# Layer 0 of a diffusion block: the last features ahead of two norms made in two token halves, each half with a norm of its own

## The chip, the cores and the metric

One core of a Trainium2 chip. The metric is device time in microseconds of one execution of the whole program, the median of the runs. The program has two parts, a two-layer transformer block on query and context tokens (the "first block") and a two-layer recurrent block; the change touches the first one alone, mostly its layer 0.

## What is computed

Query tokens `x` (256 x 1024) and context tokens `ctx` (256 x 1024), float32. Layer `l` of the first block:

```python
hx = modulate(rms_norm(x, norm_mix_g[l]), sh_a, sc_a)        # hc likewise from ctx
y_x, y_c = even_mixer(...)                                   # l = 0: two attentions
# l = 1: odd_mixer: q from hx alone, k and v from hx and hc
x = x + g_a * (y_x @ w_out[l])
x = x + g_f * swiglu(modulate(rms_norm(x, norm_ffn_g[l]), sh_f, sc_f), ffn_w_in[l], ffn_w_out[l])
# l = 0: the same two updates for ctx, with the gates and shifts of c_ctx
```

`rms_norm` divides each token by the root of the mean of its 1024 squared features, so it can begin only when the last feature of the token is there. `modulate(h, sh, sc)` is `h * (1 + sc) + sh`; all `sh`, `sc`, `g` come from a product of the condition with `mod_w` (the "modulation"), 12 column blocks of 512 per layer.

## The kernel before

**Products in three passes.** Every float32 product is made of fp32r parts: `hi*hi + hi*lo + lo*hi` (`product`, lines 505 to 509). A weight chunk is 512 inputs x 512 outputs (1 MB). SyncE loads it into `raw`, a ring of `RING = 4` slots; ScalarE writes its high part into `w_hi`, a ring of `HI_RING = 3` (line 1190); VectorE writes the low part over the raw one (line 1639). SyncE may load chunk c only when chunk c-4 is used:

```python
if c >= RING:
    sp.wait_ge(*projected.after("used", c - RING))
```

All chunks stand in one list in the order in which TensorE takes them (`lay_out`, line 2468, must name the same order as the program of TensorE). Modulation chunks are in the same list and ring; they are used raw (`mod_chunk`, line 797: one chunk of 4 kt, recorded as 8 matmuls at line 815) and need no split. `mod_row` (line 830) hangs two of them behind every second weight chunk of layer 0; `among(..., 2)` in `lay_out` is the same rule on the host side. Four modulation chunks fill one bank (5 or 6); ScalarE copies it (`modulation`, line 1340), TensorE turns it (`mod_turn`, line 781, bank 4), VectorE adds the bias (line 1870).

**Order written out by hand.** Each engine has one program. On TensorE layer 0 ends with `project_feat("w_out", 0, 2, ...)`, `root_of_squares`, `swiglu(0, 4)`, `root_of_squares`, `od_q`, `od_kv` (lines 941 to 947). A chunk of `project_feat` with all 512 tokens is 4 slabs of 128 output features x 4 kt x 3 passes = 48 matmuls with 512 columns; a slab has a PSUM bank of its own (0 to 3). Two chunks (1024 inputs) make 512 output features. `od_q` takes the 256 query tokens only (24 matmuls a chunk); `od_kv` takes 512 tokens as two groups of two token tiles. Before a product overwrites a bank, `claim` waits for the instruction that reads it last (for `od_q` and `od_kv` that is VectorE's copy in `store`, line 1927).

**The way through a norm.** For each finished slab VectorE updates the residual `X` (`residual`, lines 1891 to 1924, one 128x256 instruction for queries and one for context), ScalarE squares it (line 1219), VectorE adds the square to a sum over features (line 1674). After the last slab: `root_of_squares` (line 614) sums over the partitions, ScalarE takes the root (line 1252), VectorE the reciprocal and a diagonal matrix (lines 1690, 1691), TensorE spreads it over all partitions (line 623, bank 7). Then, per feature block k of 128 features and all 512 tokens: VectorE scales (line 1699), ScalarE applies the modulation (line 1268, twice) and writes the high part (line 1262), VectorE writes the low part (line 1704). The next product takes the blocks one by one. The low parts of weight chunks stand among this on VectorE (`lo_to`, line 1632), the high parts on ScalarE (`split_to`, line 1181), both in the order of the list.

**Names of chunks.** Around the first place: w0 to w3 are the four chunks of `w_out` (two output halves of two chunks), f0, f1, ... those of `ffn_in` (two per column block), m a modulation chunk. The last part of `ffn_out` has two output halves with one chunk of 4 kt and one of 2 kt each; q0 to q3 are the chunks of `od_q`.

## Time and profile before

| | us |
|---|---|
| median of 3 runs | 2416.76 |
| lowest, highest | 2415.67, 2419.11 |
| profiled execution | 2416.47 |
| its span, first to last instruction | 2414.7 |
| TensorE busy | 2304.4 |
| VectorE, ScalarE busy | 1503.6, 1013.3 |
| mean granted clock, share of full speed | 0.982 |

PE is TensorE, PEld its weight loads, DVE VectorE, ACT ScalarE, SPq the queue in which SyncE issues loads. A row of a timeline gives start and duration; in square brackets stands how long the engine was idle before it and whose instruction ended that. Durations of matmuls are longer than their distance, since they overlap: the distance of two starts is their cost.

### The profile page before, as it was taken

Reading aid. Unit: us, or ns where it says so; the run is one execution under the profiler, and the core shown is the slowest. Engines: PE = TensorE matmul, PEld = TensorE weight load, DVE = VectorE, ACT = ScalarE, POOL = GpSimd, SP = SyncE. Lnnn points to the kernel's source line nnn. Section 1 sums busy time; section 2 is a strip of 40 time slices with the busy share of each in tenths; the row PEclk is TensorE's granted clock in tenths of the full one; section 3 lists DMA queues with packets and bytes.
Section 4 is the critical chain, followed back from the end, with each engine's and each line's share of the span. In section 5 each row is a group of like instructions: output and inputs, shape, how many; then the busy total and the mean of one; then the engine's idle time right before and its main releaser. Section 6 shows DMA issues by size and latency. Waiting matters only on the chain.

```text
span 2414.7 us, 33051 instructions
## 1 busy us (share of the span) xinstructions
PE 2304.4 (95%) x14198; PEld 1985.0 (82%) x14198; DVE 1503.6 (62%) x1866; ACT 1013.3 (42%) x1226; POOL 0.2 (0%) x4
## 2 busy tenths in 40 slices
PE   6988989999998887999999999999999999999997
PEld 3765767777876756999999877999989988789997
DVE  3777443333356577555678767675668767767475
ACT  4255441111224155434664345443456534444343
POOL 0000000000000000000000000000000000000000
PEclk9999999999998999999999999999999999999999
DMA  8530134444332241455555453555545445445552
GB/s 324 206 143 1 54 137 176 177 172 181 133 117 93 87 105 71 158 184 192 216 191 187 174 193 143 179 188 176 189 177 205 179 174 197 148 175 177 190 176 104
DMA packets 61401, 389.19 MB, mean 161 GB/s; under 512 B 6600, under 2 KB 11080, under 8 KB 16072
## 3 DMA queue, kind: packets, MB, share of 16 engines
q1 hardware_dynamic: 61256, 387.08, 44.0%
q8 instruction: 112, 1.84, 0.3%
q14 instruction: 33, 0.27, 0.0%
HBM read 386.01 MB, written 1.05 MB: 160 GB/s over the span
## 4 chain that ended last, share of the span: by engine, by line
PE 84%; DVE 8%; ACT 4%; DMA 2%; issue 2%; SPq 0%; DVEq 0%; ACTq 0%
PE PS L507 26%; PE PS L508 25%; PE PS L509 25%; DMA raw<-chunks_in 2%; PE PS L815 1%; PE PS L984 1%; DVE w_lo L1639 1%; ACT w_hi L1190 1%; DVE stat L1838 1%; PE PS L694 1%; PE PS L966 1%; ACT xn L1268 1%; PE PS L654 1%; PE PS L719 1%; DVE BIG L1847 1%
## 5 line engine op out<-in xcount | busy, mean ns | idle before, releaser
L1639 DVE TENSOR_TENSOR w_lo<-raw,w_hi 128x2048 fp32r<-128x2048 f32 x300 | 683.5, 2290 | 514.4 <-ACT w_hi L1190 512.5
L1190 ACT ACTIVATE w_hi<-raw 128x2048 fp32r<-128x2048 f32 x300 | 571.7, 1912 | 755.7 <-PE PS L509 453.3
L507 PE MATMUL PS<-x_hi,w_hi 128*128 128x256 f32 (+1 forms) x2048 | 629.0, 307 | 12.2 <-DVE x_lo L1704 7.8
L509 PE MATMUL PS<-x_hi,w_lo 128*128 128x256 f32 (+1 forms) x2048 | 626.1, 306 | 0.0
L508 PE MATMUL PS<-x_lo,w_hi 128*128 128x256 f32 (+1 forms) x1984 | 601.5, 303 | 0.0
L507 PEld LDWEIGHTS PS<-x_hi,w_hi 128*128 128x128 f32 x2048 | 393.6, 192 | 38.5 <-issue 21.8
L509 PEld LDWEIGHTS PS<-x_hi,w_lo 128*128 128x128 f32 x2048 | 393.6, 192 | 16.7
L508 PEld LDWEIGHTS PS<-x_lo,w_hi 128*128 128x128 f32 x1984 | 381.7, 192 | 14.1
L507 PE MATMUL PS<-w_hi,x_hi 128*128 128x512 f32 (+1 forms) x800 | 318.5, 398 | 23.2 <-DVE x_lo L1704 12.0
L508 PE MATMUL PS<-w_lo,x_hi 128*128 128x512 f32 (+1 forms) x800 | 314.5, 393 | 0.0
L509 PE MATMUL PS<-w_hi,x_lo 128*128 128x512 f32 (+1 forms) x800 | 313.9, 392 | 0.0
L507 PE MATMUL PS<-BIGR,w_hi 128*128 128x256 f32 (+1 forms) x896 | 272.8, 304 | 0.0
L508 PE MATMUL PS<-BIGR,w_hi 128*128 128x256 f32 (+1 forms) x896 | 272.3, 304 | 0.0
L509 PE MATMUL PS<-BIGR,w_lo 128*128 128x256 f32 (+1 forms) x896 | 272.3, 304 | 0.0
L507 PEld LDWEIGHTS PS<-w_hi,x_hi 128*128 128x128 f32 x800 | 152.6, 191 | 63.2 <-issue 18.8
L507 PEld LDWEIGHTS PS<-BIGR,w_hi 128*128 128x128 f32 x896 | 171.3, 191 | 10.4 <-issue 3.6
L509 PEld LDWEIGHTS PS<-w_hi,x_lo 128*128 128x128 f32 x800 | 152.5, 191 | 31.8
L508 PEld LDWEIGHTS PS<-w_lo,x_hi 128*128 128x128 f32 x800 | 152.6, 191 | 29.7
L509 PEld LDWEIGHTS PS<-BIGR,w_lo 128*128 128x128 f32 x896 | 171.3, 191 | 6.9
L508 PEld LDWEIGHTS PS<-BIGR,w_hi 128*128 128x128 f32 x896 | 171.3, 191 | 6.7
L507 PE MATMUL PS<-w_hi,BIGR 128*128 128x512 f32 x192 | 75.7, 394 | 0.0
L509 PE MATMUL PS<-w_hi,BIGR 128*128 128x512 f32 x192 | 74.8, 390 | 0.0
(298 smaller groups left out, 2281.2 us busy)
## 6 DMA issues: line engine op xcount, KB each, us to landing
raw<-chunks_in SPq DMA_DIRECT2D x348, 1024.0 KB, 4.8
bias_ring<-brows_in SPq DMA_DIRECT2D x32, 256.0 KB, 5.1
G<-nrows_in SPq DMA_DIRECT2D x2, 1536.0 KB, 6.6
free_b<-rel_in SPq DMA_DIRECT2D x4, 512.0 KB, 7.8
BIG<-rel_in SPq DMA_DIRECT2D x4, 512.0 KB, 8.7
tabt<-tabs_in SPq DMA_DIRECT2D x1, 1536.0 KB, 12.6
X<-x_in SPq DMA_DIRECT2D x1, 1024.0 KB, 8.7
X<-ctx_in SPq DMA_DIRECT2D x1, 1024.0 KB, 10.7
```

The costliest lines, as they stand in the source:

```text
L507: pe.matmul(o, lhs[0], rhs[0], start=start, stop=False, **more)
L508: pe.matmul(o, lhs[0], rhs[1], start=False, stop=False, **more)
L509: return pe.matmul(o, lhs[1], rhs[0], start=False, stop=stop, **more)
L654: mm = pe.transpose(PS[:, bank, t * P:(t + 1) * P], src(b, t), ident)
L694: mm = pe.matmul(PS[:, s + i, 0:d["nk"]], a, b, start=m == 0, stop=m == len(mats) - 1)
L719: mm = pe.matmul(PS[:, b, 0:P], pT_, val, start=j == 0, stop=j == n - 1)
L815: mm = pe.matmul(PS[32 * kt:32 * kt + 32, b, :], cond[:, 4 * kg + kt, at:at + 32], w[:, kt, :], start=first, stop=i == last and kg == 1, s ...
L966: mm = pe.matmul(PS[:, b, cols], qkT[:, 8 + 2 * h + j, s * P:(s + 1) * P], qkT[:, 2 * h + j, s * P:256], start=j == 0, stop=j == 1)
L984: mm = pe.matmul(PS[:, 6 + t, 0:dv], lhs, val[:, s, h * dv:(h + 1) * dv], start=s == 0, stop=s == len(blocks) - 1)
L1190: act.activation(w_hi[:, i % HI_RING, :], ring[:, n % RING, :], ACT.Copy).then_inc(*hi_ready.now(n))
L1268: ins = act.activation(o, o, ACT.Identity, bias=modc[l][:, kind * 8 + k, w:w + 1], scale=modc[l][:, kind * 8 + 8 + k, w:w + 1])
L1639: dve.tensor_tensor(w_lo[:, c % RING, :], ring[:, c % RING, :], w_hi[:, i % HI_RING, :].bitcast(F32), ALU.subtract).then_inc(*lo_ready.now(c))
```

## The change

Both places, end of `w_out` into `ffn_in` and end of `ffn_out` into `od_q`, are treated alike. The last 512 output features are made for the query tokens first (banks 0, 1) and then for the context tokens (banks 5, 6), from the same two chunks, which are held until both are done. Each half has its own squares, sum, root and spread (banks 7 and 4, two columns and 256 columns), its own scaling and its own high and low parts. The first column block of `ffn_in` is made for the queries, block by block, then for the context, again from held chunks; `od_q` begins with the query blocks, and the second group of `od_kv` waits for the context blocks. Scale, reciprocal root and low part are now two VectorE instructions of 256 columns with the modulation's factor in them, the high part one ScalarE instruction. In the first place the modulation chunks are moved: four behind w1 and four behind f3, instead of two behind w1, w3, f1 and f3. The low half of `y4T`, `krT` and a buffer of modulation rows lie elsewhere, and `ffn_in` reads its activations from other memory.

The core of the diff (order and names; left out are the new buffers' places, the semaphore counters and waits that follow from these):

```diff
-        y4T = pair_of((xhi_, xnr_), 512, KD)
+        y4T = pair_of((xhi_, bigr(8192, 4096)), 512, KD)
+        hT_f0 = pair_of((xlo_, xnr_), 512, KD)
...
+            def project_halves(st, j, rhs, k_tiles, hooks):
+
+                parts, held = range(-(-k_tiles // KC)), []
+                for who in range(2):
+                    for kg in parts:
+                        if who == 0:
+                            held.append(take_chunk(st, 0))
+                        c, w = held[kg]
+                        for s in range(4):
+                            bank, at = half_banks[who][s // 2], s % 2 * 256
+                            if kg == 0 and at == 0:
+                                claim(bank)
+                            for kt in range(KC * kg, min(KC * kg + KC, k_tiles)):
+                                mm = product(PS[:, bank, at:at + 256], [a[:, kt - KC * kg, s * P:(s + 1) * P] for a in w],
+                                             [a[:, kt, who_cols(who)] for a in rhs], kt == 0 and at == 0, kt == k_tiles - 1, True)
+                            if kg == parts[-1] and at:
+                                mm.then_inc(*projected.now(st, 0, j, (who, s // 2)))
+                                reader[bank] = x_ready.after(st, 0, j, (who, s // 2))
+                            elif who == 1 and s == 3:
+                                mm.then_inc(*projected.now(("chunk", c)))
+                            if who == 1 and s == 3:
+                                used(c)
+                            if (who, kg, s) in hooks:
+                                hooks[who, kg, s]()
+                plan[("last chunk", st, 0, j)] = c
...
+            def first_halves(st, rhs, tiles_of, freed, hooks):
+
+                held = []
+                claim(0, 1, 2, 3)
+                for who in range(2):
+                    for kg in range(2):
+                        if who == 0:
+                            held.append(take_chunk(st, 0))
+                        c, w = held[kg]
+                        for kt in range(KC * kg, KC * kg + KC):
+                            pe.wait_ge(*copied_v.after(tiles_of, (who, kt)))
+                            for s in range(4):
+                                mm = product(PS[:, s, who_cols(who)], [a[:, kt - KC * kg, s * P:(s + 1) * P] for a in w],
+                                             [a[:, kt, who_cols(who)] for a in rhs], kt == 0 and who == 0, kt == KD - 1, True)
+                                if who == 1 and kt == KD - 1:
+                                    mm.then_inc(*projected.now(st, 0, 0, s))
+                                    reader[s] = freed(0, s)
+                            if who == 1 and kt == KC - 1:
+                                mm.then_inc(*projected.now(("chunk", c)))
+                            if (who, kt) in hooks:
+                                hooks[who, kt]()
+                        if who == 1:
+                            used(c)
+                plan[("last chunk", st, 0, 0)] = c
...
+            def half_sums(key, who):
+
+                acc, bank = sums[4][0], (7, 4)[who]
+                pe.wait_ge(*x_summed.after(key, (who, KD - 1)))
+                claim(bank)
+                for t in range(2):
+                    mm = pe.matmul(PS[:, bank, t:t + 1], acc[:, (2 * who + t) * P:(2 * who + t + 1) * P], tab("ones")[:, 0:1],
+                                   start=True, stop=True)
+                mm.then_inc(*sums_bc.now(key, who))
+
+            def half_spread(key, who):
+
+                bank = (7, 4)[who]
+                pe.wait_ge(*rstd_diag.after(key, who))
+                pe.matmul(PS[:, bank, 256:512], tab("ones"), sums[4][2][0][:, who_cols(who)], start=True,
+                          stop=True).then_inc(*rstd_bc.now(key, who))
+                reader[bank] = scaled.after(key, who, KD - 1)
...
+            def mod_four(kg):
+
+                for _ in range(4 * kg):
+                    mod_chunk()
...
+                    if halves:
+                        first_halves("ffn_in", hT_f0, ("ffn", 0), freed,
+                                     {(0, 1): lambda: half_sums(("ffn", 0), 1), (0, 3): lambda: half_spread(("ffn", 0), 1)})
+                        tiles_of = None
+                        project_feat("ffn_in", 0, 1, hT_f0, n0=1, between=mod_four, width=width, freed=freed)
...
+                        project_feat("ffn_out", 0, 1, ffT[0], n0=2 * part, k_tiles=2 * n, width=width, freed=updated("ffn_out", 0),
+                                     need=lambda kg: hidden.after("ffn", 0, 2 * n0 + min(KC * kg + KC, 2 * n) - 1))
+                        project_halves("ffn_out", 2 * part + 1, ffT[0], 2 * n,
+                                       {(1, 0, 1): lambda: half_sums(("mix", 1), 0), (1, 0, 3): lambda: half_spread(("mix", 1), 0)})
+                        continue
...
-            project_feat("w_out", 0, 2, y4T, width=512, freed=updated("w_out", 0), need=copied("y0"), between=mod_row)
-            mod_end(0, 2)
-            root_of_squares(("ffn", 0), 4)
+            project_feat("w_out", 0, 1, y4T, width=512, freed=updated("w_out", 0), need=copied("y0"), between=mod_four)
+            project_halves("w_out", 1, y4T, KD,
+                           {(0, 1, 0): lambda: mod_end(0, 2), (1, 0, 1): lambda: half_sums(("ffn", 0), 0),
+                            (1, 0, 3): lambda: half_spread(("ffn", 0), 0)})
             swiglu(0, 4)
-            root_of_squares(("mix", 1), 4)
-            project_tok("od_q", 1, 2, KD, tokens(hT[4]), 1, tiles_of=("mix", 1))
-            project_tok("od_kv", 1, 4, KD, tokens(hT[4]), 2)
+            mix = ("mix", 1)
+            project_tok("od_q", 1, 1, KD, tokens(hT[4]), 1, tiles_of=mix)
+            project_tok("od_q", 1, 1, KD, tokens(hT[4]), 1, n0=1,
+                        between=lambda kg: half_sums(mix, 1) if kg == 0 else half_spread(mix, 1))
+            project_tok("od_kv", 1, 4, KD, tokens(hT[4]), 2, need_second=lambda: copied_v.after(mix, (1, KD - 1)))
...
+            def half_high(key, to, who, k0, k1):
+
+                l, kind = key[1], 0 if key[0] == "mix" else 3
+                for k in range(k0, k1):
+                    act.wait_ge(*scaled.after(key, who, k))
+                    act.activation(to[0][:, k, who_cols(who)], full[4][:, k, who_cols(who)], ACT.Identity,
+                                   bias=modc[l][:, kind * 8 + k, who:who + 1]).then_inc(*copied_s.now(key, who, k))
...
-            for k in range(KD):
-                act.wait_ge(*x_ready.after("w_out", 0, k // 4, k % 4))
+            for k in range(4):
+                act.wait_ge(*x_ready.after("w_out", 0, 0, k))
                 square(("ffn", 0), 4, k)
-                if k == 3:
-                    split_to(first + 3)
-                    split_to(first + 4)
             modulation(3)
-            root_mod(("ffn", 0), 4)
-            norm_mod(("ffn", 0), 4, 2, lambda: split_to(first + 5))
+            split_to(first + 3)
+            split_to(first + 4)
+            ffn = ("ffn", 0)
+            half_squares(ffn, "w_out", 1, 0)
+            act.wait_ge(*mods_ready.after(0, 2))
+            half_root(ffn, 0)
+            split_to(first + 5)
+            half_high(ffn, hT_f0, 0, 0, 2)
+            half_squares(ffn, "w_out", 1, 1, (0,))
+            half_high(ffn, hT_f0, 0, 2, 4)
+            half_squares(ffn, "w_out", 1, 1, (1,))
+            half_high(ffn, hT_f0, 0, 4, 6)
+            half_root(ffn, 1)
+            half_high(ffn, hT_f0, 0, 6, 8)
+            split_to(first + 6)
+            half_high(ffn, hT_f0, 1, 0, 8)
             swiglu(0, 4)
-            for k in range(KD):
-                if k % 4 == 0:
-                    split_for("ffn_out", 0, 4 + k // 4)
-                act.wait_ge(*x_ready.after("ffn_out", 0, 4 + k // 4, k % 4))
-                square(("mix", 1), 4, k)
-            root_mod(("mix", 1), 4)
-            norm_mod(("mix", 1), 4, 0)
+            mix, first_od = ("mix", 1), place_of[plan["first chunk", "od_q", 1]]
+            for k in range(4):
+                if k == 0:
+                    split_to(first_od - 2)
+                act.wait_ge(*x_ready.after("ffn_out", 0, 4, k))
+                square(mix, 4, k)
+            split_to(first_od)
+            half_squares(mix, "ffn_out", 5, 0)
+            act.wait_ge(*mods_ready.after(1, 0))
+            half_root(mix, 0)
+            split_to(first_od + 1)
+            half_high(mix, hT[4], 0, 0, 4)
+            split_to(first_od + 2)
+            half_high(mix, hT[4], 0, 4, 8)
+            half_squares(mix, "ffn_out", 5, 1)
+            split_to(first_od + 3)
+            half_root(mix, 1)
+            split_to(first_od + 4)
+            half_high(mix, hT[4], 1, 0, 8)
...
+                def scale(k):
+                    dve.scalar_tensor_tensor(full[4][:, k, cols], X[:, who, k, :], modc[l][:, kind * 8 + 8 + k, who:who + 1], r,
+                                             ALU.mult, ALU.mult).then_inc(*scaled.now(key, who, k))
+
+                if k0 == 0:
+                    dve.wait_ge(*rstd_bc.after(key, who))
+                    dve.wait_ge(x_ready.sem, x_ready.count)
+                    scale(0)
+                for k in range(k0, k1):
+                    if k + 1 < KD:
+                        scale(k + 1)
+                    dve.wait_ge(*copied_s.after(key, who, k))
+                    dve.scalar_tensor_tensor(to[1][:, k, cols], full[4][:, k, cols], modc[l][:, kind * 8 + k, who:who + 1],
+                                             to[0][:, k, cols].bitcast(F32), ALU.add, ALU.subtract).then_inc(*copied_v.now(key, (who, k)))
...
-            steps = {(0, 0): 12, (1, 0): 13, (1, 1): 14}
-            residual("w_out", 0, 2, 0, ("ffn", 0), lambda j, i: lo_to(ev + steps.get((j, i), 0)))
-            norm_mod(("ffn", 0), 4, 2, (0, 2), lambda k: lo_to(ev + 15) if k == 5 else None)
-            swiglu(0, 4, ("mix", 1))
-            norm_mod(("mix", 1), 4, 2, None, lambda k: lo_for("ffn_out", 0, 5) if k == 3 else None)
+            first = place_of[plan["first chunk", "w_out", 0]]
+            ffn, mix = ("ffn", 0), ("mix", 1)
+            residual("w_out", 0, 2, 0, ffn, lambda j, i: lo_to(first + 2), 1)
+            lo_to(first + 3)
+            half_update(ffn, "w_out", 1, 2, 0, 0)
+            half_adds(ffn, 0, 0)
+            modulation(0, 2)
+            lo_to(first + 4)
+            half_update(ffn, "w_out", 1, 2, 0, 1)
+            half_adds(ffn, 0, 1)
+            half_diag(ffn, 0)
+            half_low(ffn, hT_f0, 0, 0, 1)
+            lo_to(first + 5)
+            half_low(ffn, hT_f0, 0, 1, 2)
+            half_update(ffn, "w_out", 1, 2, 1, 0)
+            half_adds(ffn, 1, 0)
+            half_low(ffn, hT_f0, 0, 2, 3)
+            half_update(ffn, "w_out", 1, 2, 1, 1)
+            half_low(ffn, hT_f0, 0, 3, 4)
+            half_adds(ffn, 1, 1)
+            half_low(ffn, hT_f0, 0, 4, 6)
+            half_diag(ffn, 1)
+            half_low(ffn, hT_f0, 0, 6, 8)
+            half_low(ffn, hT_f0, 1, 0, 4)
+            lo_to(first + 6)
+            half_low(ffn, hT_f0, 1, 4, 8)
+            swiglu(0, 4, mix)
+            first_od = place_of[plan["first chunk", "od_q", 1]]
+            lo_to(first_od - 1)
+            half_update(mix, "ffn_out", 5, 5, 0, 0)
+            half_adds(mix, 0, 0)
+            lo_to(first_od)
+            half_update(mix, "ffn_out", 5, 5, 0, 1)
+            half_adds(mix, 0, 1)
+            half_diag(mix, 0)
+            half_low(mix, hT[4], 0, 0, 4)
+            lo_to(first_od + 1)
+            half_low(mix, hT[4], 0, 4, 8)
+            lo_to(first_od + 2)
+            for b in range(2):
+                half_update(mix, "ffn_out", 5, 5, 1, b)
+                half_adds(mix, 1, b)
+            lo_to(first_od + 3)
+            half_diag(mix, 1)
+            lo_to(first_od + 4)
+            half_low(mix, hT[4], 1, 0, 8)
...
-        among(weight_chunks(i["w_out"][l]), 2)
+        if l == 0:
+            w_out = weight_chunks(i["w_out"][0])
+            chunks.append(w_out[0:2])
+            mod_next(4)
+            chunks.append(w_out[2:4])
+        else:
+            chunks.append(weight_chunks(i["w_out"][1]))
         n0 = 0
         for n in FF_PARTS[l]:
-            among(weight_chunks(paired(i["ffn_w_in"][l])[:, 512 * n0:512 * (n0 + n)]), 2)
+            w_in = weight_chunks(paired(i["ffn_w_in"][l])[:, 512 * n0:512 * (n0 + n)])
+            if l == 0 and n0 == 0:
+                chunks.append(w_in[0:4])
+                mod_next(4)
+                w_in = w_in[4:]
+            among(w_in, 2)
             among(weight_chunks(i["ffn_w_out"][l][256 * n0:256 * (n0 + n)]), 2)
             n0 += n

```

`half_update`, `half_adds`, `half_diag`, `half_squares` and `half_root` are the steps of the norm above for one half: two updates, two adds, reciprocal and diagonal of 256 columns, two squares, one root of two columns.

## Rows read from the trace of the kernel before

**Rows 1.** The page, part 1: busy time of each engine.

```profile
PE 2304.4 (95%) x14198; PEld 1985.0 (82%) x14198; DVE 1503.6 (62%) x1866; ACT 1013.3 (42%) x1226; POOL 0.2 (0%) x4
```

**Rows 2.** Stretches of 20 us: PE, PEld, DVE, ACT, POOL busy, PEclk, DMA share, GB/s.

```profile
320.00:340.00 20.00, 12.28 (x54) 8.99 (x47) 11.46 (x22) 14.73 (x27) 0.00 (x0) 0.74 0.38 155
720.00:740.00 20.00, 9.73 (x28) 6.64 (x27) 13.27 (x25) 12.47 (x24) 0.00 (x0) 0.66 0.14 53
```

**Rows 3.** Whom TensorE waited for: us in total, times, longest.

```profile
PE PS L507 <- DVE x_lo L1704: 19.8, 5, 5.5
```

**Rows 4.** TensorE in order of time, end of `w_out`: start, us, what.

```profile
318.75 1.92 PE L815 MATMUL PS<-raw,bias_ring 128*32 128x512 f32 x16
...
331.59 0.77 PE L507 MATMUL PS<-x_hi,w_hi 128*128 128x512 f32 x1 [5.24 <-DVE x_lo L1704]
...
336.31 0.39 PE L509 MATMUL PS<-x_hi,w_lo 128*128 128x512 f32 x1
```

**Rows 5.** The chain that ended last, 270 to 420 us: start, us, what.

```profile
294.94 1.85 PE PS L815 x16
...
307.98 4.77 DMA raw<-chunks_in
...
355.75 1.85 PE PS L815 x16
...
379.63 1.85 PE PS L815 x16
381.49 0.43 PE PS L507
```

**Rows 6.** TensorE in order of time, end of `ffn_out`, start of `od_q`.

```profile
720.66 0.39 PE L509 MATMUL PS<-BIGR,w_lo 128*128 128x512 f32 x1
...
735.26 0.77 PE L507 MATMUL PS<-w_hi,x_hi 128*128 128x512 f32 x1 [4.29 <-DVE x_lo L1704]
...
744.89 0.47 PE L507 MATMUL PS<-w_hi,x_hi 128*128 128x512 f32 x1 [2.21 <-DVE x_lo L1704]
```

**Rows 7.** VectorE in order of time, `od_q` and `od_kv` being stored.

```profile
763.13 1.22 DVE L1935 COPY BIG<-PS 128x1024 f32<-128x1024 f32 x1 [1.14 <-PE PS L509]
...
833.14 2.35 DVE L1935 COPY BIG<-PS 128x1024 f32<-128x1024 f32 x2
```

**Rows 8.** TensorE at the last `od_kv` column block.

```profile
834.50 0.77 PE L507 MATMUL PS<-w_hi,x_hi 128*128 128x512 f32 x1 [6.13 <-DVE BIG L1935]
```

**Rows 9.** Weight splits, from the page's part 5: xcount, busy, mean ns.

```profile
L1639 DVE TENSOR_TENSOR w_lo<-raw,w_hi 128x2048 fp32r<-128x2048 f32 x300 | 683.5, 2290 | 514.4 <-ACT w_hi L1190 512.5
L1190 ACT ACTIVATE w_hi<-raw 128x2048 fp32r<-128x2048 f32 x300 | 571.7, 1912 | 755.7 <-PE PS L509 453.3
```

**Rows 10.** Chunk loads of 104 to 108 us, asked by line.

```profile
L1154 SPq DMA_DIRECT2D raw<-chunks_in x2: 328/328/328, 105.1 to 106.1; - x2
...
DMA to landing us min/median/max: 4.9/5.8/6.6
```

**Rows 11.** One modulation chunk on TensorE, same stretch.

```profile
105.00 1.07 PE L815 MATMUL PS<-raw,bias_ring 128*32 128x512 f32 x8
```

**Rows 12.** The split that waited for the second of those loads.

```profile
112.74 1.92 ACT L1190 ACTIVATE w_hi<-raw 128x2048 fp32r<-128x2048 f32 x1 [5.66 <-DMA raw<-chunks_in]
```

**Rows 13.** TensorE, matmuls of 512 columns back to back.

```profile
341.99 0.39 PE L507 MATMUL PS<-x_hi,w_hi 128*128 128x512 f32 x1
...
349.92 0.39 PE L509 MATMUL PS<-x_hi,w_lo 128*128 128x512 f32 x1
```

**Rows 14.** TensorE, matmuls of 256 columns back to back.

```profile
979.78 0.28 PE L507 MATMUL PS<-x_hi,w_hi 128*128 128x256 f32 x1
...
983.98 0.28 PE L509 MATMUL PS<-x_hi,w_lo 128*128 128x256 f32 x1
```

**Rows 15.** VectorE, residual update of 128x256, two instructions.

```profile
316.93 0.87 DVE L1910 SCALAR_TENSOR_TENSOR X<-PS,bias_ring,X 128x256 f32<-128x256 f32 x2
```

**Rows 16.** ScalarE, affine step of 128x256, four instructions.

```profile
328.13 2.07 ACT L1268 ACTIVATE xn<-xn,bias_ring 128x256 f32<-128x256 f32 x4 [4.05 <-DVE small L1889]
```

More of the change, by code:

```diff
@@ L541, in project_tok @@
                                 for kt in range(KC * kg, min(KC * kg + KC, k_tiles)):
+                                    if tiles_of == ("mix", 1) and j == n0 and t == 0:
+                                        pe.wait_ge(*copied_v.after(tiles_of, half(kt)))
                                     mm = product(PS[:, 2 * pair + t, 0:width], lhs(kt, 2 * g + t),
@@ L920, in swiglu, with freed @@
                 for part, n in enumerate(FF_PARTS[l]):
-                    project_feat("ffn_in", l, n, hT[tiles], n0=n0, tiles_of=tiles_of, between=between, width=width,
-                                 freed=lambda j, i: (unit_acted if i < first_u else stored).after("ffn_in", l, j, i))
+                    halves = l == 0 and part == 0
+                    def freed(j, i):
+                        return (unit_acted if i < first_u else stored).after("ffn_in", l, j, i)
+                    if halves:
[3 more added lines that the diff above has]
+                        project_feat("ffn_in", 0, 1, hT_f0, n0=1, between=mod_four, width=width, freed=freed)
+                    project_feat("ffn_in", l, n - 2 * halves, hT[2] if l else hT_f0, n0=n0 + 2 * halves, tiles_of=tiles_of, between=between,
+                                 width=width, freed=freed)
                     last = part == len(FF_PARTS[l]) - 1
@@ L1253, in root_mod, with half_squares, half_root @@
                                scale=1.0 / D).then_inc(*std_ready.now(key))
+            def half_squares(key, st, j, who, banks=(0, 1)):
+                for b in banks:
+                    act.wait_ge(*x_ready.after(st, 0, j, (who, b)))
+                    for k in (4 + 2 * b, 5 + 2 * b):
+                        act.wait_ge(*x_summed.after(key, k - 2 if b == 0 else (who, k - 2)))
+                        act.activation(sums[4][2][k % 2][:, who_cols(who)], X[:, who, k, :],
+                                       ACT.Square).then_inc(*x_squared.now(key, (who, k)))
+            def half_root(key, who):
+                act.activation(stat[:, 20:21], eps, ACT.Sqrt)
+                act.wait_ge(*sums_bc.after(key, who))
+                act.activation(stat[:, 2 * who:2 * who + 2], PS[:, (7, 4)[who], 0:2], ACT.Sqrt, bias=eps,
+                               scale=1.0 / D).then_inc(*std_ready.now(key, who))
+            def half_high(key, to, who, k0, k1):
[4 more added lines that the diff above has]
+                                   bias=modc[l][:, kind * 8 + k, who:who + 1]).then_inc(*copied_s.now(key, who, k))
             def norm_mod(key, tiles, part, middle=None):
@@ L1717, in norm_mod, with half_update @@
                         at_tile(k)
+            def half_update(key, st, j, kind, who, b):
+                dve.wait_ge(*projected.after(st, 0, j, (who, b)))
+                for s in range(2):
+                    k = 4 + 2 * b + s
+                    ins = dve.scalar_tensor_tensor(X[:, who, k, :], PS[:, half_banks[who][b], 256 * s:256 * s + 256],
+                                                   gate(0, kind, k, who), X[:, who, k, :], ALU.mult, ALU.add)
+                ins.then_inc(*x_ready.now(st, 0, j, (who, b)))
@@ new lines, in half_adds, with half_diag @@
+            def half_adds(key, who, b):
+                acc, _, sq = sums[4]
+                for k in (4 + 2 * b, 5 + 2 * b):
+                    dve.wait_ge(*x_squared.after(key, (who, k)))
+                    dve.wait_ge(*x_summed.after(key, 3 if k == 4 else (who, k - 1)))
+                    o = acc[:, who_cols(who)]
+                    dve.tensor_tensor(o, o, sq[k % 2][:, who_cols(who)], ALU.add).then_inc(*x_summed.now(key, (who, k)))
+            def half_diag(key, who):
+                dve.wait_ge(*std_ready.after(key, who))
+                r = stat[:, 4 + 2 * who:6 + 2 * who]
+                link(dve.reciprocal(r, stat[:, 2 * who:2 * who + 2]))
+                dve.tensor_tensor(sums[4][2][0][:, who_cols(who)].rearrange("p (t d) -> p t d", t=2),
+                                  ident.unsqueeze(1).to_broadcast([P, 2, P]), r.unsqueeze(2).to_broadcast([P, 2, P]),
+                                  ALU.mult).then_inc(*rstd_diag.now(key, who))
@@ L1897, in residual @@
                 before = []
-                for j in range(2):
+                for j in range(n):
                     for i in range(2 if l else 4):
@@ L1964, in swiglu @@
                         modulation(1, 0)
-                    if part == len(FF_PARTS[l]) - 1:
+                    if part == len(FF_PARTS[l]) - 1 and l == 0:
+                        first_od = place_of[plan["first chunk", "od_q", 1]]
+                        residual("ffn_out", 0, 5, 2 * part, key, lambda j, i: lo_to(first_od - 2), 1)
+                    elif part == len(FF_PARTS[l]) - 1:
                         residual("ffn_out", l, 5, 2 * part, key)
```

22 lines of the change are left out of this document (16 added, 6 removed).

## The prediction, made before the changed kernel ran

> **What bounds the kernel now.** The page says that TensorE is busy 95% of the span [rows 1]: what a stage is worth is the time for which TensorE stands still in it, or runs at half clock. The stretches of 20 us show two holes beside this change, at 320 and at 720 us, with 12.3 and 9.7 us of work at a granted clock of 0.74 and 0.66 [rows 2]. The view of waits names the releaser: VectorE's low half of the normed activations, 19.8 us in 5 waits [rows 3]. The timelines give the sizes. *First hole:* `w_out` and its two modulation chunks end at 320.7, the first `ffn_in` matmul starts at 331.6, and the next ten run at 0.43 us each, which is 1.2 GHz, where 0.227 is 2.4 GHz; they are through at 336.3 [rows 4, 13]. That is 10.9 us of standstill and 2.0 lost to the clock, **12.9**. *Second hole:* `ffn_out` ends at 720.9, `od_q` starts at 735.3 (14.4 us), pauses again before 744.9 (2.2 to 2.4 us), and both restarts pay some 1.8 for the clock [rows 6]: **20.4**.
>
> **What it costs in matmuls.** The last 512 features of each stage and the first `ffn_in` block go over 256 tokens at a time. 36 matmuls of 512 columns take 7.93 us from the first start to the last, 0.227 each [rows 13], 36 of 256 columns 4.20 us, 0.120 each [rows 14]. A split costs 2 x 0.120 - 0.227 = 0.013 us, for 96 + 96 + 72 = 264 matmuls: 3.4 us, 2.5 of them in the first stage. The Trainium skill ("TensorE: Matmul & The Clock Gate", Back-to-back issue gap) gives 518 cycles for 512 columns and 262 for 256, with which the split would cost 0.0025 us each and 0.7 in all. The rows decide.
>
> **The moved modulation chunks, first place.** Before, the order is w0 w1 m m w2 w3 m m f0 f1 m m f2 f3 m m f4. After, it is w0 w1 m m m m w2 w3 f0 f1 f2 f3 m m m m f4. The raw ring has four slots, so a load is issued when the chunk four places earlier is used. With T the end of w1 (294.9, [rows 5]), the fourth m is issued at T (its slot is w1's) and w2 only when the first m is done. Exactly this pair of loads exists in the trace: a chunk ends at 105.0, one load goes out at 105.1, a modulation chunk takes 1.07 us, the next load goes out at 106.1, and the second needs 6.6 us, since it shares the engines with the first: the split that waits for it starts at 112.74, 7.7 after the first chunk's end [rows 10 to 12]. So w2 lands at T+7.7, ScalarE's high part takes 1.91 and VectorE's low part 2.29 [rows 9], T+11.9. Behind this low part, by the new order, VectorE has the first residual update, 0.87 [rows 15], which frees PSUM bank 0: w2 starts at **T+12.8**. Before, it started at T+1.9 (two mods, 294.94 + 1.85). Four mods take 3.8 us, the rest TensorE stands, and I charge one restart at half clock, 2.0 as at 331.6. A single load without a queue lands after 4.77 us [rows 5]. The Trainium skill ("DMA: Bandwidth & Descriptors", Anatomy of one DMA) has about 2.0 us plus bytes over 436 GB/s, by which an estimate for the second of two 1 MiB loads is 6.8 us after the first's issue instead of 7.6; each restart would then come 0.8 earlier.
>
> **From w2 to the end of f1.** ScalarE splits w2 before it squares, VectorE updates four banks behind w2's low part (about 5.2 us with the adds), and only then comes w3's split: squares done T+16.3, mod row copied 16.9, high 18.8, low T+21.1. TensorE needs w3 at T+20.5: 0.7 lost. Query half of w3 done T+27.7 (with the modulation turn, 0.9, inside). VectorE meanwhile has the update, two adds, the modulation and f0's low part (2.29) ahead of the second update, so the query squares are summed at T+31.9, while the sum wants to start two slabs into the context half, T+30.5: 1.4 lost. The spread of the inverse roots comes two slabs later and waits for nothing; small products are 0.3 and 0.65 per half. The query half of the norm now runs beside the context half of w3, as it should: per feature block 2 VectorE instructions of 0.4 [rows 15] and one ScalarE of 0.52 [rows 16], block 0 ready at T+38.0, when TensorE is free at T+41.4. So **the hole of 12.9 goes**. What is late next: the context sums. VectorE has f1's low part, both context updates, adds and four query blocks ahead of them: T+46.4, wanted at T+44.2: 2.2 lost. After that each block is ready before its turn. Sum of the stretch T to the start of f2: 12.8 + 2.0 + 0.7 + 1.4 + 2.2 + 46.1 (384 half matmuls) + 2.8 (small products) = 68.0, T+68.0. Before it is 355.75 + 1.85 = 357.6 [rows 5], T+62.7. **+5.3 us.** The removed hole and four mods (16.7) are paid back by the w2 wait.
>
> **Second place.** f2 and f3 take 21.8, then come four mods again, with F the end of f3: the fourth issued at F, f4 at F+1.1, landed F+7.7, ready F+11.9. Before, two mods: F+1.9 [379.63 to 381.49, rows 5]. **+10.0**, and a restart at half clock, **+2.0**. ScalarE and VectorE wait for f4 in order ahead of the SiLU and product of block 1, but these are done by F+13, before bank 2 is wanted. First stage: 5.3 + 12.0 = **+17.3**. From f4 on TensorE is bound by itself, so nothing of this is made up.
>
> **Third place, `ffn_out` to `od_q`.** Here no modulation chunk is left. The residual of the first half no longer waits behind the low part of the last chunk, w3's counterpart is ready at 710.3 for a use at 710.2. The query sums are 2.1 us late (q0's low part sits between the two updates), TensorE ends `ffn_out` at 724.7 instead of 720.9, and goes on at once: query blocks come ahead of `od_q`, whose first pass ends at 735.6 and second at 747.2, the spread at 747.8. Hole of 20.4 gone. But a new wait: `od_kv` claims banks 0 and 1, which hold `od_q`'s first block, and VectorE stores that only behind all eight context blocks (8 x 0.8 + 0.6 from the spread on): 755.0 + 1.2 for the copy = 756.2. TensorE stands **8.5 us**, plus 2.0 at half clock. Its first `od_kv` chunk ends at 769.2. Before: the last `od_q` store at 763.1 [rows 7] follows the end of `od_q`, plus 10.9: 774.0. **-4.8.** Downstream the last `od_kv` block waits 6.13 us for a store [rows 8] that is behind the key norm on VectorE [rows 7]; that chain begins when the second `od_kv` block is done, so it moves with TensorE by the same 4.8. If it moves less, the gain is 3; were the 2.0 not paid, 7.
>
> **Sum.** The profiled execution is 2416.47, its span 2414.7, the median of the runs 2416.76. 2416.5 + 17.3 - 4.8 = 2429.0; to the median 0.3 more. I say **2429**. Unknown: what short stops (0.7, 1.4, 2.2, 2.1 us) do to the clock. The nearest row is the stop before 744.9, which cost 1.8: from 0 to 4 x 1.8 = 7.
>
> **Rivals.** *A (0.60):* as above, 2424 to 2434. *B, clock (0.17):* the short stops each cost a spell of 1.2 GHz: 2429 + 7 = 2436. For it: the 2.2 us stop before 744.9. *C, the small surplus (0.13):* VectorE is faster through the norm halves than I count, the late sums (0.7 + 1.4 + 2.2 + 2.1) vanish and the wait for the store halves (4.2 + clock 2): 2429 - 12.6 = 2416 to 2421; this is within 0.2% of before. *D, faster (0.10):* the loads behind the mods are hidden after all, because they go out before the first m is used. Then w2 starts at T+3.8 + 0.9 and f4 at F+3.8: 8.1 + 8.1 us less, and 4.0 of clock, 2409. It decides at one point: whether w2 and f4 can be issued at T and F or before. Against it: slot and program order, and the pair at 105 us.
>
> **Numbers.** About 0.2% (4.8 us) is what a measurement can tell from no change. Faster by more than it has D: 0.10. Within it, C and part of A's edge: 0.12. Slower: 0.78. The range leaves out D and the tails of B: 2417 to 2438.
>
> **What would show it.** TensorE waiting for a low weight part some 9 us at about 298 to 307 and again near 387 to 396, with ScalarE's split behind a DMA; after `od_q` a wait of about 8 us for a VectorE copy; no wait for x_lo over 1 us. It is wrong if the two waits behind the mods are under 4 us, or if the first stage (end of w1 to start of f4, 86.6 us now) is not some 17 longer.

## The result, and the profile after

| | before | after |
|---|---|---|
| median, us | 2416.23 | 2433.93 |
| single runs | 2415.67, 2415.69, 2416.76, 2419.11 | 2429.62, 2431.58, 2436.29, 2437.04 |
| profiled execution | 2416.47 | 2429.62 |
| its span | 2414.7 | 2427.8 |

The changed kernel takes 1.007 times as long (95% interval 1.0058 to 1.0082): slower by 17.7 us. The forecast was 2429, with a range of 2417 to 2438. A fourth run of the kernel before is counted here, so its median is 2416.23 and not the 2416.76 of its first three.

Part 1 of the page after; the counterpart is [rows 1]:

```profile
PE 2307.9 (95%) x14466; PEld 2000.0 (82%) x14466; DVE 1510.5 (62%) x1910; ACT 1005.3 (41%) x1222; POOL 0.2 (0%) x4
```

TensorE is busy 3.5 us longer, with 268 matmuls more. The profiled execution is 13.2 us longer, so the greater part of that is standstill, and the waits tell more. Whom TensorE waited for after (us in total, times, longest), against [rows 3]:

```profile
PE PS L514 <- DVE w_lo L1791: 15.0, 10, 5.0
PE PS L514 <- DVE BIG L2134: 14.4, 2, 8.3
PE PS L896 <- DMA raw<-chunks_in: 11.7, 6, 5.5
...
PE PS L514 <- DVE x_lo L1856: 7.7, 2, 5.2
...
PE PS L662 <- DVE G L1887: 6.5, 3, 2.5
...
PE PS L514 <- DVE X L2109: 5.7, 1, 5.7
```

The waits for the normed activations are gone from both places; what is left of `x_lo` stands at the start of the kernel (5.2) and in the next layer (2.6). In their place stand a weight low part (5.0), a residual update (5.7), two modulation chunks that wait for a load (4.5 of the 11.7; the other 7.1 stand in the first 60 us, as the 7.2 of the kernel before do), sums of squares (6.5), and VectorE's copy of `od_q` out of PSUM (8.3).

**The wait behind the first four modulation chunks.** TensorE in order of time (start, us, what, idle before):

```profile
291.49 2.78 PE L896 MATMUL PS<-raw,bias_ring 128*32 128x512 f32 x24
296.64 1.94 PE L896 MATMUL PS<-raw,bias_ring 128*32 128x512 f32 x8 [2.37 <-DMA raw<-chunks_in]
304.23 0.55 PE L514 MATMUL PS<-x_hi,w_hi 128*128 128x256 f32 x1 [5.66 <-DVE X L2109]
```

and the chain that ended last through the same stretch (start, us, what):

```profile
291.56 1.04 PE PS L896 x8
...
292.62 6.43 DMA raw<-chunks_in
...
299.07 1.92 ACT w_hi L1295
...
301.01 0.04 DVE w_lo L1791
...
303.22 0.88 DVE X L2109 x2
```

Read it from the bottom: w2 begins when the first residual update has freed its bank; the update stands behind w2's low part on VectorE; that waits for the high part, this for the load, and the load begins at 292.62, when the *first* modulation chunk is used, not at 291.56. The row of w2's low part (`w_lo`) is short because the chain leaves it at once: VectorE works on it from 301.01 for 2.29 us, and the update follows at 303.22. The fourth modulation chunk, issued at 291.59 into w1's slot, is itself late by 2.4 us, and takes 1.94 instead of 1.07, since the granted clock is half from 296.7. Behind w2's start the clock stays at half to 310.3: 28 matmuls of 256 columns run at 0.213 us each, where 0.120 is full speed. Before, the same point had 1.9 us of modulation between w1 and w2 and no wait (the first row of [rows 5] is this modulation).

**The same at the second four.** The chain again; here f4 waits for its own low part, and begins at 395.28:

```profile
383.65 1.04 PE PS L896 x8
...
384.71 6.26 DMA raw<-chunks_in
...
390.99 1.92 ACT w_hi L1295
...
392.93 2.30 DVE w_lo L1791
...
395.28 0.80 PE PS L514
```

**Third place.** TensorE waits for the sums of the query half, and then at the start of `od_kv`:

```profile
734.62 0.61 PE L662 MATMUL PS<-tabt,G 128*128 128x1 f32 x4 [2.51 <-DVE G L1887]
...
773.34 0.76 PE L514 MATMUL PS<-w_hi,x_hi 128*128 128x512 f32 x1 [8.26 <-DVE BIG L2134]
...
847.19 0.77 PE L514 MATMUL PS<-w_hi,x_hi 128*128 128x512 f32 x1 [6.13 <-DVE BIG L2134]
```

The last row is the wait that the kernel before has too [rows 8]. VectorE shows why the wait at 773.34 is 8.3 us: it is busy with the context blocks and copies `od_q` only behind the last of them.

```profile
765.12 0.87 DVE L1904 SCALAR_TENSOR_TENSOR xn<-X,bias_ring,PS 128x256 f32<-128x256 f32 x2 [2.40 <-PE PS L670]
...
771.57 0.48 DVE L1915 SCALAR_TENSOR_TENSOR x_lo<-xn,bias_ring,x_hi 128x256 fp32r<-128x256 f32 x1 [0.18 <-ACT x_hi L1381]
771.97 1.22 DVE L2134 COPY BIG<-PS 128x1024 f32<-128x1024 f32 x1
```

**Where the time went.** Three marks stand in every trace: T, the end of w1 (where two modulation chunks were moved ahead of w1, less their 1.9 us); M, the start of the modulation chunks behind f5; K, the first matmul of the last `od_kv` block [rows 8].

| | T | T to M | M to K |
|---|---|---|---|
| before | 294.9 | 108.6 | 431.1 |
| after | 291.5 | 127.6 | 428.2 |
| spread, first place | 292.9 | 121.9 | 430.1 |
| spread, second place | 294.0 | 117.6 | 429.8 |
| spread, both | 293.6 | 114.2 | 430.0 |
| third place alone | 294.7 | 108.7 | 431.4 |
| `od_q` stored early | 295.4 | 129.3 | 425.8 |
| low parts later | 297.2 | 125.1 | 425.9 |
| all repairs | 294.7 | 109.0 | 420.8 |
| third place alone, repaired | 293.6 | 109.6 | 420.9 |

After against before: +19.0 and -2.9, and from K to the end +0.4. The profiled execution also reached T 3.4 us earlier; T scatters from 291.5 to 297.2 over kernels that differ only behind it (the changed one, second place, `od_q` stored early, low parts later), so I count that as scatter and not as the change. Without it the sum is +16.5, close to the +17.7 of the medians; the single execution (+13.2) flatters the change.

### The profile page after: what moved, and what is told of

Its sections match the earlier page's. It is cut to its first block, busy times and chain, and to the rows that moved or that the text cites. A ratio compares the mean times of both kernels' runs of the same rounds, so it can differ in the third digit from the quotient of the medians.

```text
span 2427.8 us, 33640 instructions
## 1 busy us (share of the span) xinstructions
PE 2307.9 (95%) x14466; PEld 2000.0 (82%) x14466; DVE 1510.5 (62%) x1910; ACT 1005.3 (41%) x1222; POOL 0.2 (0%) x4
## 4 chain that ended last, share of the span: by engine, by line
PE 82%; DVE 9%; ACT 4%; DMA 2%; issue 2%; SPq 0%; DVEq 0%; ACTq 0%
PE PS L514 25%; PE PS L515 25%; PE PS L516 25%; DVE w_lo L1791 2%; ACT w_hi L1295 1%; DMA raw<-chunks_in 1%; PE PS L1089 1%; PE PS L896 1%; DVE stat L2037 1%; PE PS L1071 1%; PE PS L775 1%; PE PS L735 1%; PE PS L800 1%; DVE BIG L2046 1%; DVE PS L2035 0%
## 5 line engine op out<-in xcount | busy, mean ns | idle before, releaser
L514 PE MATMUL PS<-x_hi,w_hi 128*128 128x256 f32 (+1 forms) x1728 | 496.6, 287 | 12.6 <-DVE X L2109 5.7
L516 PE MATMUL PS<-x_hi,w_lo 128*128 128x256 f32 (+1 forms) x1728 | 494.7, 286 | 0.0
L515 PE MATMUL PS<-x_lo,w_hi 128*128 128x256 f32 x1632 | 463.0, 284 | 0.0
L514 PEld LDWEIGHTS PS<-x_hi,w_hi 128*128 128x128 f32 x1728 | 334.1, 193 | 17.1 <-issue 8.0
L516 PEld LDWEIGHTS PS<-x_hi,w_lo 128*128 128x128 f32 x1728 | 333.9, 193 | 1.3
L515 PEld LDWEIGHTS PS<-x_lo,w_hi 128*128 128x128 f32 x1632 | 314.5, 193 | 0.4
L515 PE MATMUL PS<-BIGR,w_hi 128*128 128x256 f32 (+1 forms) x1016 | 308.3, 303 | 0.0
L514 PE MATMUL PS<-BIGR,w_hi 128*128 128x256 f32 (+1 forms) x920 | 277.4, 301 | 0.1
L515 PEld LDWEIGHTS PS<-BIGR,w_hi 128*128 128x128 f32 x1016 | 195.6, 193 | 7.1
L514 PEld LDWEIGHTS PS<-BIGR,w_hi 128*128 128x128 f32 x920 | 175.9, 191 | 9.6 <-issue 3.4
L515 PE MATMUL PS<-xn_r,w_hi 128*128 128x512 f32 (+1 forms) x448 | 162.1, 362 | 0.0
L514 PE MATMUL PS<-x_lo,w_hi 128*128 128x512 f32 (+1 forms) x384 | 145.4, 379 | 5.0 <-DVE w_lo L1791 5.0
```

Source lines behind the costliest of these rows:

```text
L514: pe.matmul(o, lhs[0], rhs[0], start=start, stop=False, **more)
L515: pe.matmul(o, lhs[0], rhs[1], start=False, stop=False, **more)
L516: return pe.matmul(o, lhs[1], rhs[0], start=False, stop=stop, **more)
```

## The experiments

The theory: the four-slot ring makes w2 and f4 late behind four modulation chunks, this costs about 10 us at each place, and the third place pays for its removed hole with the wait for the `od_q` copy. The main rivals: the split matmuls and short stops are the cost, or the third place is a clear gain by itself.

**1. Modulation chunks spread, first place.** Two behind w0 and two behind w1, so that at most two stand ahead of w2. (`mod_four` gives four modulation chunks behind the second weight chunk, the new `mod_two` two behind each.)

```diff
-            project_feat("w_out", 0, 1, ..., between=mod_four)
+            project_feat("w_out", 0, 1, ..., between=mod_two)
...
-            chunks.append(w_out[0:2])
-            mod_next(4)
+            chunks.append(w_out[0:1])
+            mod_next(2)
+            chunks.append(w_out[1:2])
+            mod_next(2)
```

> The changed kernel, but the four modulation chunks at the first place stand as two behind w0 and two behind w1. Theory (load order): w2's slot is then free one chunk earlier, its load is out before w1 begins, w2 starts 2 us after w1's end instead of 12.7, without a spell at half clock; w3 is now the one that waits, some 1.5 us, because its slot is w1's. Worth 9 to 10 us: about 2424 as a median, 2420 in a run like the profiled one. Rival (VectorE's order of low parts, updates and adds bounds this stage): under 3 us gained, the stops only move.

Measured: 2426.87 (4 runs, ratio to before 1.0039, 1.0023 to 1.0054), 7.1 less than the changed kernel; in the trace 5.7 (T to M). The wait of w2 went as told, the rest came back one chunk later, where w3 waits instead and half clock follows (TensorE, idle before in brackets):

```profile
298.20 0.36 PE L514 MATMUL PS<-x_hi,w_hi 128*128 128x256 f32 x1 [1.50 <-DVE X L2114]
306.35 0.39 PE L514 MATMUL PS<-x_hi,w_hi 128*128 128x256 f32 x1 [2.16 <-DVE w_lo L1796]
```

In the changed kernel w3 has no wait, because w2 itself is late: the wait was covered by the other one. The expectation had w3's wait (1.5 us); it had neither the 1.5 us that w2 still waits nor the half clock behind w3 (307.2 to 314.0, which costs 3.4).

**2. The same, second place.** Two behind f2 and two behind f3.

```diff
-                        project_feat("ffn_in", 0, 1, hT_f0, n0=1, between=mod_four, ...)
+                        project_feat("ffn_in", 0, 1, hT_f0, n0=1, between=mod_two, ...)
...
-                chunks.append(w_in[0:4])
-                mod_next(4)
+                chunks.append(w_in[0:3])
+                mod_next(2)
+                chunks.append(w_in[3:4])
+                mod_next(2)
```

> The changed kernel, but the four modulation chunks at the second place stand as two behind f2 and two behind f3. Theory (load order): f4 starts some 2 us after f3's end instead of 11.7, the spell at half clock behind it goes; with the two chunks that now stand earlier that is 9.5 to 10 us: about 2424 as a median, 2420 in a run like the profiled one. Rival (the first place's delay has put ScalarE and VectorE behind, f4 is late anyway): under 3 us gained.

Measured: 2425.55 (5 runs, 1.0036, 1.0023 to 1.0048), 8.4 less than the changed kernel; T to M is 10.0 shorter. f4 has no wait left and nothing comes back behind it.

**3. Both.** The two edits together.

> Both places spread as two and two. Theory: the gains add, 19 to 20 us, so 2412 to 2415 and thus at or just under the kernel before (2416): the two waits behind the modulation chunks are the whole loss. Rival (other costs of the halves: 264 more matmuls, short stops at half clock, the wait for the store): it stays over 2420.

Measured: 2418.97 (11 runs, 1.0009, 1.0 to 1.0018), 15.0 less than the changed kernel, near the sum of the two alone, 15.4. It misses my 2412 to 2415 by 4: w2 and w3 still wait 1.6 and 2.2 us, and the clock is half from 308.2 to 315.0. Four modulation chunks in a row instead of two and two are thus some 15 of the 17.7 us. The chain shows that a load is still the first cause at w2, but an earlier one:

```profile
282.56 1.90 PE PS L896 x16
...
284.48 9.31 DMA raw<-chunks_in
...
293.82 1.93 ACT w_hi L1300
```

Three loads are asked within 2 us here, two of modulation chunks and then w2's, and the last takes 9.3 us. A wait of 1.6 us stays where there were 5.7.

**4. The third place alone.** `w_out`, its norm and the whole of the first `ffn_in` part as before; only `ffn_out` into `od_q` in halves.

```diff
-            project_feat("w_out", 0, 1, y4T, width=512, ..., between=mod_four)
-            project_halves("w_out", 1, y4T, KD, ...)
+            project_feat("w_out", 0, 2, y4T, width=512, ..., between=mod_row)
+            mod_end(0, 2)
+            root_of_squares(("ffn", 0), 4)
...
-                    halves = l == 0 and part == 0
+                    halves = False
```

> Only the third place (ffn_out to od_q) is changed; w_out, its norm, ffn_in and the order of the chunks are as before. Theory: 2.9 us under the kernel before, as the two traces show between the end of the last ffn_in chunk and the last od_kv block (the prediction had 4.8): 2413 to 2414. Rival: the third place gives nothing by itself, since the wait for the store and its half clock eat it: 2415.5 to 2417.5.

Measured: 2417.14 (11 runs, 1.0001, 0.9993 to 1.001). The gain of 2.9 is not there: M to K is 0.3 longer than before. Its wait for the `od_q` copy is that of the changed kernel; what differs is the clock behind the query sums. The stretch of TensorE first, then ten us behind the stop for the sums in windows (us, PE, PEld, DVE, ACT, POOL busy, PEclk, DMA share, GB/s):

```profile
718.94 1.01 PE L662 MATMUL PS<-tabt,G 128*128 128x1 f32 x4 [2.52 <-DVE G L1875]
...
760.39 0.77 PE L514 MATMUL PS<-w_hi,x_hi 128*128 128x512 f32 x1 [8.25 <-DVE BIG L2122]
```

```profile
720.00:730.00 10.00, 10.00 (x57) 9.69 (x58) 3.74 (x10) 3.98 (x6) 0.00 (x0) 0.74 0.36 113
```

and the ten us behind the same stop in the changed kernel:

```profile
735.00:745.00 10.00, 10.00 (x69) 9.32 (x69) 5.80 (x12) 6.13 (x10) 0.00 (x0) 1.00 0.53 185
```

After the same stop of 2.5 us the one runs at half clock up to 725.2, the other doesn't. From the matmuls behind this stop to the end of TensorE's next idle time it is 27.0 us here and 24.3 there (718.94 to 745.97, 734.62 to 758.90), so the spell costs some 2.7. The three spread kernels have M to K at 429.8 to 430.1, between the two. So by itself, as written, the third place is worth nothing: a hole of 20.4 us [rows 6] is paid back by an 8.3 us wait, the restarts and the late sums.

**5. `od_q` stored ahead of the context blocks.** Both column blocks are copied as soon as they are done; the low part of a later weight chunk, which used to stand ahead of the copy, follows (the last argument, `False`, leaves it out of `store`).

```diff
             half_diag(mix, 1)
+            nq_part = lambda j, g: nq[:, :, j * 512:(j + 1) * 512]
+            store("od_q", 1, 1, 1, nq_part, 0, False)
             lo_to(first_od + 4)
+            store("od_q", 1, 1, 1, nq_part, 1, False)
             half_low(mix, hT[4], 1, 0, 8)
-            store("od_q", 1, 2, 1, lambda j, g: nq[:, :, j * 512:(j + 1) * 512])
+            lo_for("od_q", 1, 1)
```

> The changed kernel, with VectorE's two copies of od_q put ahead of the low halves of the context blocks (in front of them stands only what od_q itself needs). Theory (the claim of banks 0 and 1 is the wait): the first group of od_kv goes on at once at the spread, the second waits some 3 us for the context blocks, which come 1 us later; the stop of 8.3 us and most of its half clock go, 6 to 8 us: 2426 to 2428 as a median against 2434. Rival (the context blocks are the real limit, the bank only stands beside them): under 3 us.

Measured: 2433.38 (4 runs, 1.0072, 1.0056 to 1.0087). A miss: the median is that of the changed kernel. The trace has the wait gone and two small ones in its place:

```profile
781.22 0.79 PE L514 MATMUL PS<-w_hi,x_hi 128*128 128x512 f32 x1 [2.25 <-DVE x_lo L1915]
...
800.57 0.47 PE L514 MATMUL PS<-w_hi,x_hi 128*128 128x512 f32 x1 [1.24 <-DVE BIG L2134]
```

M to K is 425.8, that is 2.3 less than after, and 4.2 less than the 430.0 of the spread kernels; the stop of 2.51 us before 740.3 has half clock behind it, up to 746.8, which the same stop of the changed kernel has not. In the first stage this trace is 1.7 longer (f4 waited 7.2 us instead of 5.0). Four runs each, over 2429.6 to 2437.0 for the changed kernel, don't resolve 2 to 4 us, so what the early store is worth by itself was not settled. It was not measured on top of experiment 3 either.

**6. Low parts later.** In both places the low part of the next chunk stands behind the diagonal of the query half, and no longer between its two updates.

```diff
-            lo_to(first + 4)
             half_update(ffn, "w_out", 1, 2, 0, 1)
             half_adds(ffn, 0, 1)
             half_diag(ffn, 0)
+            lo_to(first + 4)
...
-            lo_to(first_od)
             half_update(mix, "ffn_out", 5, 5, 0, 1)
             half_adds(mix, 0, 1)
             half_diag(mix, 0)
+            lo_to(first_od)
```

> The changed kernel, with VectorE's low part of f0 and of q0 moved from between the two query updates to behind the reciprocal root, where VectorE stands idle for the spread. Theory: the query sums come 2.3 us earlier at both places, the stops of 1.6 and 2.5 us go, 4 us, and up to 3 us of half clock behind each in those runs that have it: 2426 to 2430 as a median. Rival (the stop is set by update, squares and adds themselves): under 1.5 us, since 128x256 updates, squares and adds alone take 2.2 us.

Measured: 2430.39 (4 runs, 1.0057, 1.0044 to 1.0071), 3.5 less than the changed kernel. The stops for the query sums fall from 1.62 to none and from 2.51 to

```profile
735.65 0.61 PE L662 MATMUL PS<-tabt,G 128*128 128x1 f32 x4 [0.32 <-DVE G L1887]
```

T to M is 2.5 shorter, M to K 2.3. The lowest run of the changed kernel (2429.62) lies among these four, so the medians alone don't show the gain; the stops in the trace do.

**7. All of it.** Experiments 3, 5 and 6 together, and the context sums and spread of the first place asked for behind the fifth and seventh query block instead of the second and fourth.

```diff
-                                     {(0, 1): lambda: half_sums(("ffn", 0), 1), (0, 3): lambda: half_spread(("ffn", 0), 1)})
+                                     {(0, 4): lambda: half_sums(("ffn", 0), 1), (0, 6): lambda: half_spread(("ffn", 0), 1)})
```

> All mends together: modulation chunks two and two at both places, copies of od_q early, low parts later, and the context sum and its spread of the ffn norm three blocks later. Theory: from e3 (2419.0) another 6 to 8, 4 and 2.4 us, and less half clock: 2402 to 2407. Rival (the clock falls after what is left, w3's wait and the small products, and eats half): 2409 to 2413.

Measured: **2404.67** (5 runs, 0.9954, 0.9942 to 0.9967): 29.3 less than the changed kernel, 11.8 less than the one before. T to M is 109.0, where it was 108.6 before the change; M to K is 10.2 shorter than before. What the later context sums give by themselves was not measured.

```profile
755.23 0.50 PE L514 MATMUL PS<-w_hi,x_hi 128*128 128x512 f32 x1 [2.25 <-DVE x_lo L1920]
774.58 0.47 PE L514 MATMUL PS<-w_hi,x_hi 128*128 128x512 f32 x1 [1.10 <-DVE BIG L2139]
...
824.50 0.76 PE L514 MATMUL PS<-w_hi,x_hi 128*128 128x512 f32 x1 [6.14 <-DVE BIG L2139]
```

**8. The third place alone, repaired.** Experiment 4 with the early store and the later low part (the parts of 5 and 6 that lie in the third place).

> The third place alone changed, with copies of od_q early and q0's low part later; the first stage as in the kernel before. Theory: from the third place alone (2417.1) the stop of 2.5 us with its spell of half clock (2.9) and 6 to 8 us of the wait for the store go: 2404 to 2407, clearly under the kernel before. Rival: VectorE's two norms of od_q and od_kv behind it bound this stage, so only 3 us come through: 2413 to 2415.

Measured: 2406.81 (5 runs, 0.9962, 0.995 to 0.9975). Against experiment 4 that is 10.3 us for two moved steps on VectorE, and almost all that experiment 7 gains. The first stage in halves, even repaired, is worth 2.1 us between these two medians (their runs overlap: 2404.1 to 2407.0 and 2405.8 to 2410.8), and nothing against the stage before: T to M is 109.0 in experiment 7, 108.6 before, 109.6 here. Its hole of 12.9 us is gone there, but w2 and w3 wait 1.2 and 2.2, the half clock from 308.9 to 315.7 costs 3.4, and with the forecast's 2.5 for the split matmuls and 2.8 for the small products that is 12.1 us, nearly what the hole was worth. Experiment 7 keeps the buffers where the change put them and is the fastest, so their new places are not what made the change slow.

## Why the prediction was right

**The loads behind the modulation chunks** were the cause, as told. w2 starts at T+12.7 (told 12.8), f4 at F+11.7 (11.9); the load takes 6.43 and 6.26 us from the first modulation chunk's end, where the pair at 105 us gave 6.6 [rows 10]. Experiments 1 to 3 take this away and get 15.0 us back. One thing the forecast did not have: the wait at w2 comes in two pieces, 2.4 ahead of the fourth modulation chunk and 5.7 behind it, which changes nothing in the sum, since w2's own load ends later. The formula that I weighed stands in the Trainium skill ("DMA: Bandwidth & Descriptors", Anatomy of one DMA) for transfers that GpSimd issues, while these go out from SyncE; it would have each restart 0.8 earlier. The trace after lies between, nearer the row: from the first issue of the pair to the second landing it is 7.5 us at the first place and 7.3 at the second, where the row gave 7.6 and the formula 6.8.

**The split matmuls.** TensorE's busy time grew by 3.5, told 3.4 for the split. Half clock and small products are in this number too, so it agrees with the term and doesn't measure it. At full clock the split matmuls come every 0.120 us in the changed kernel (339.82 to 340.90), as in [rows 14].

**First stage, T to M:** +19.0 against +17.3. The mis-sized term is the stretch up to f2, which starts at T+70.3 where I said T+68.0. The restart of w2 lost 2.6 to the clock (told 2.0), the w3 wait was absent (told 0.7), both sums were 0.2 later than told (1.62 and 2.36 for 1.4 and 2.2), and the stop for the context sums had half clock behind it (341.0 to 344.5), which cost some 1.6 and which I had left to the range. That makes 1.9 of the 2.3; the remaining 0.4 I can't place. From F to M the second place came out at +11.6, told 12.0, so that the stage as a whole is off by less than its first stretch.

**Third place, M to K:** -2.9 against -4.8. The wait for the `od_q` copy is 8.26 (told 8.5), the half clock behind it 4.4 us long and so 2.2 (2.0), the query sums 2.51 (2.1), and `od_kv` starts at 773.34; less the 15.6 carried over from the first two places (VectorE's product of the feed-forward part at 701.3 stood at 685.7 before) that is 757.7, where 756.2 was told. These 1.5 us are most of the missing 1.9: 0.4 is the longer stop for the query sums, 0.6 a wait for a weight's low part before 758.90 that I had not told, the rest I can't place. The gain was told too large by 1.9, and by 5.1 in experiment 4, where there is a spell of half clock behind the query sums.

**Rival B, the clock,** was partly true. Of the stops told as 0.7, 1.4, 2.2 and 2.1 only the third had a spell in the profiled execution, but other kernels had it behind the fourth, and the runs of 2436.3 and 2437.0 lie at B's 2436. That the high runs are high through such spells is argued by analogy, no trace shows it. Their granted clock is 0.979 and 0.978, that of the other two 0.980; but in the kernel before a run of 2414.9 has 0.979 and one of 2419.3 has 0.981, so the mean clock does not sort the runs, and the scatter of the runs stays unexplained. **Rival C** is refuted by the waits for the sums, each 0.2 to 0.4 later than told, **rival D** by the issue at 292.6: the load goes out behind the first modulation chunk.

The point forecast was 4.9 below the median. The two terms above make 3.6 of it, and what is left is within the scatter of single runs. In the chances one number does not fit: C alone has 0.13, but no change from before, which holds C and a part of A, was given 0.12.

## What to carry to other kernels

Where all loads go through one ring, the order of the chunks is also the order of the loads: cheap chunks in a row use up the ring's lead, since a chunk of 1.07 us frees a slot in a tenth of the time that a load and two splits need (6.3 + 1.9 + 2.3). In this kernel spreading four in a row to two and two gave back 7.1 us at one place and 8.4 at the other. Two in a row left no wait at the second place; at the first, w2 and w3 still waited 1.6 and 2.2 us. When a norm is cut in halves, look at the in-order engine next: the first half's sums must not queue behind a weight split, nor a copy that frees a bank behind the second half; in the third place these two steps made the difference between no gain and 10 us. And a hole that is removed is worth only what the new order doesn't ask for in its place: in the first place that was all of it.

## What the runs showed of the hardware

- A stop of TensorE by 2.2 to 2.5 us is followed by a granted clock of half in some traces and not in others, though TensorE's program is the same up to there: none behind 2.51 us before 734.6 in the changed kernel, half clock up to 746.8 behind 2.51 before 740.3 in experiment 5; none behind 2.36 before 335.3 in experiment 1, 335.5 to 342.3 behind 2.36 before 335.9 in experiment 3. Experiment 4 has it behind 2.52, up to 725.2. In experiments 4 and 5 the clock was down (from 718.4 and 740.0) before the engine went on; it may also fall a little after the stop (at 341.0 after a stop that ended at 339.0). What decides was not found.
- Loads of 1 MB asked close together landed one behind the other. In the changed kernel four were asked from 291.6 to 294.3 and landed at 296.6, 299.0, 301.5 and 304.0: 5.0, 6.4, 8.1 and 9.7 us after each one's own issue, where one alone takes 4.8 [rows 5]. In experiment 3 three asked within 2 us took 4.8, 7.7 and 9.3. So each load in the queue ahead adds 1.4 to 2.9 us.
